# Two transformer blocks on one core: the plain sum of squares at the block boundary moved from VectorE to GpSimd

## The chip, the cores and the metric

The kernel runs on one core of one Trainium2 chip. The metric is the device time of one execution in microseconds, and the time of a kernel is the median of its runs. The trace comes from one further, profiled execution of the same program.

## The reference, cut to what matters

The program computes two blocks in a row on a sequence of 1024 tokens with 1024 features. The first ends with an MLP and a final norm; its output goes straight into the first norm and the input projection of the second:

```python
def first_block(x, ..., final_norm_g):
    ...
        x = x + jnp.square(jax.nn.relu(h2 @ w_up[l])) @ w_down[l]
    return rms_norm(x, final_norm_g)

def second_block(x, norm1_g, w_in, b_in, ...):
    ...
        h = _rmsnorm(x, norm1_g[l])
        z = h @ w_in[l] + b_in[l]
        q, k, v, c_a, c_b, g_a, g_b = jnp.split(z, splits, axis=-1)
        ...
```

Two norms thus stand one behind the other. With r1 the inverse root of the mean of x², the first gives y = x · r1 · final_norm_g, and the second needs the mean of y², which is r1² times the mean of x² · final_norm_g². Each token needs two sums over the features: one of the plain squares x², and one of the squares weighted by final_norm_g².

## The kernel before

**Layout.** Activations are kept with features on the 128 partitions and tokens along the free axis: `x_t` is eight slices (`KT` = 8) of 128 features by 1024 tokens. A weight tile is 128 output features of a matrix. All products are float32 split in two parts (`hi` and `lo`, three matmuls for each pair), so one weight tile against one activation slice is 3 x 2 matmuls of 128x512, and a whole tile is 48. `product(n, slot, first_bank, ...)` on TensorE is one such tile; it waits until GpSimd has split tile `n` (`weight_split`) and ends by raising `tile_done`.

**Weights.** SyncE loads tile `n` into `w_raw` slot n mod 2. GpSimd's `split` makes `w_hi` with a cast (line 975) and `w_lo` with a subtraction (line 983), and waits beforehand for `tile_done` at n - 1, since the tile two back must have left the slot. `weight_stream` writes out the order of all tiles for both of them: a part of it is a list of tiles written out, then a hardware loop (`Fori`), then another list. Tiles `T_CB` to `T_CB + 3` (`CT` = 4) are the first of the second block; before, they are a hardware loop of two rounds with two tiles each.

**Squares at the boundary.** ScalarE squares the eight slices of `x_t` in the order `BLOCK_ORDER`: square 0 goes straight into `sq_sum`, squares 1 to 4 into `sq`, 5 to 7 into `sq_rest`; each raises `sq_ready`. VectorE then adds in this order, 15 instructions of 128x1024:

- `sum_gained(0, 0)`: `sq_sum_gain` = square 0 times its weight (line 3055). It must read `sq_sum` before that is overwritten.
- `sum_plain(e, ...)` for e = 1 to 7: `sq_sum` += square e (line 3049).
- `sum_gained(e, ...)` for e = 1 to 7: `sq_sum_gain` += square e times its weight (line 3058).

Each raises `sq_summed`, and each waits for the one before it, since the sum is in place.

**TensorE at the boundary.** `sum_features` multiplies a sum by a matrix of ones, two float32 matmuls of 128x512 (line 1140), which adds over the partitions. The order is written by hand:

```python
            product(T_CB + 1, 1, 2, h_hi, h_lo, range(KT // 2))
            sum_features(sq_sum, SUMS_MIX2 + KT, 4)
            product(T_CB + 1, 1, 2, h_hi, h_lo, range(KT // 2, KT))
            sum_features(sq_sum_gain, SUMS_MIX2 + 2 * KT - 1, 6)

            pe.wait_ge(mean_log, 3)
            product(T_CB + 2, 0, 4, h_hi, h_lo)
            pe.wait_ge(block_mean, 1)
            product(T_CB + 3, 1, 6, h_hi, h_lo)
```

The plain sum goes to banks 4 and 5, where ScalarE takes its logarithm (line 2231, `mean_log`), from which it makes the inverse roots; the weighted sum goes to banks 6 and 7, and VectorE multiplies it in at line 3076 (`block_mean`). Engines run their own instructions in program order, so a wait of TensorE holds everything behind it.

Of the kernel before, what the change touches and what calls it, by code (L numbers as in the profile page):

```python
# [26 lines left out]
ACT = mybir.ActivationFunctionType  # L27
# [162 lines left out]
SUMS_MIX1 = 0  # L190
SUMS_MLP = SUMS_MIX1 + 2 * (KT - 1)
SUMS_MIX2 = SUMS_MLP + KT - 1
SUMS_FFN = SUMS_MIX2 + 2 * KT - 1
SUMS_OUT = SUMS_FFN + KT - 1


# [13 lines left out]
def two_blocks(nc, dram, out):  # L210
    ctx = ExitStack()
    with ctx:
# [253 lines left out]
        def by_group(tile):  # L466
# [160 lines left out]
         product_added, product_taken) = (q_gate, f_ready, kd_start, g_gate, qd_start, v_ready, kd_turned, kd_tok_ready,  # L627
                                          update_done, o_done, o_sq)
        group_joined = [o_mean, o_inv]
        factors_loaded, direct_loaded, rest_loaded, sums_loaded = (x_loaded[j:j + 2] for j in range(0, KT, 2))  # L630

        block = ctx.enter_context(nc.Block())
# [41 lines left out]
        def weight_stream(eng, step, step_pair, mlp_down, begun=0):  # L674

            parts = [
                ((pool_tiles + head_tiles(0))[begun:], HEADS - 1, lambda i: head_tiles(i + 1), []),  # L680
                ([columns(dram["w_out"], d * P) for d in ORDER], 0, None, []),
                (mlp, mlp_up),
                (mlp_down,),
                ([], CT // 2, lambda i: [columns(w_in2, CB2 + i * 2 * P + j * P) for j in range(2)], []),
                (pair_tiles(0)[0:2], PAIRS - 1, lambda p: pair_tiles(p)[2:4] + pair_tiles(p + 1)[0:2],
                 pair_tiles(PAIRS - 1)[2:4] + gate_tiles(0)),
                ([], KT - 1, lambda i: gate_tiles(i + 1), []),
                ([], KT // 2, lambda i: [branches(i * 2 * P + j * P) for j in range(2)], []),
                ([columns(dram["w_out_2"], d * P) for d in ORDER], 0, None, []),
                (ffn, ffn_up),  # L690
                (ffn_down(0), FFN_CHUNKS - 2, lambda i: ffn_down(i + 1), ffn_down(FFN_CHUNKS - 1)),
            ]
            n, skipped = begun, 0
            for part in parts:
                if len(part) == 1:
                    part[0]()
                    continue
                if len(part) == 2:

                    stage, tiles = part  # L700
                    assert (n, skipped) == (stage.tile, stage.skipped)
                    for q in range(2):
                        step_pair(stage, n, stage.pair + q, q, tiles(q))
                        n += 2
                    with eng.Fori(0, stage.pairs // 2 - 1) as i:
                        for s in range(2):
                            step_pair(stage, i * 4 + (n + 2 * s), i * 2 + (stage.pair + 2 + s), s, tiles(i * 2 + (2 + s)))
                    n += 2 * stage.pairs - 4
                    skipped += 16 * stage.pairs
                    continue  # L710
                ahead, count, body, behind = part
                for halves in ahead:
                    step(n, n % 2, halves, skipped)
                    n += 1
                if count:
                    size = len(body(0))
                    assert size % 2 == 0 and n % 2 == 0
                    with eng.Fori(0, count) as i:
                        for j, halves in enumerate(body(i)):
                            step(i * size + (n + j), j % 2, halves, skipped)  # L720
                    n += count * size
                for j, halves in enumerate(behind):
                    step(n, n % 2, halves, skipped)
                    n += 1
            assert n == T_END
# [28 lines left out]
        def join_corner(eng, g, j):  # L754

            rest, corner = down_sum(g, j, "t1"), output_at(g, j, "c22")
            if j == 0:
                eng.wait_ge(sums_loaded[g], 16 + 96)
            eng.tensor_tensor(rest, rest, corner, ALU.add).then_inc(group_joined[g], 1)
            eng.wait_ge(group_joined[g], HEADS + 12 + 2 * j + 1)  # L760
            eng.tensor_tensor(rest, rest, down_sum(g, j, "t3"), ALU.add).then_inc(group_joined[g], 1)

        def joined_before(j, name):

# [169 lines left out]
        def _(pool):  # L934
# [7 lines left out]
            def split(n, slot, _, skipped):  # L942

                pool.wait_ge(weight_loaded[slot], arrived(n, slot, skipped))
                hi, lo = w_hi[:, slot, :], w_lo[:, slot, :]
                if isinstance(n, int) and n == T_END - 1:

                    pool.wait_ge(tile_done, T_END - 4)
                    hi, lo = w_hi_last[:, :], w_lo_last[:, :]
                elif isinstance(n, int) and n == T_HEADS:  # L950

                    pool.wait_ge(x_turned, 2 * KT)
                    hi, lo = w_hi_first[:, :], w_lo_first[:, :]
                elif isinstance(n, int) and n == T_OUT1 + 1:

                    pool.wait_ge(tile_done, n - 1)
                    pool.wait_ge(level_moved, (HEADS - 1) * LEVELS + 3)
                elif isinstance(n, int) and n in (T_OUT1 + 2, T_OUT1 + 3):

                    pool.wait_ge(mix_split, KT - 1)  # L960
                    for read in ((k_ready, q_ready), (v_turned, sg_ready))[n - T_OUT1 - 2]:
                        pool.wait_ge(read, HEADS)
                    hi, lo = w_out_parts[n - T_OUT1 - 2]
                elif isinstance(n, int) and n == T_DOWN2:

                    pool.wait_ge(tile_done, n - 2)
                elif isinstance(n, int) and n == T_DOWN2 + 1:

                    pool.wait_ge(tile_done, T_DOWN2)
                elif not isinstance(n, int) or n >= 2:  # L970

                    pool.wait_ge(tile_done, n - 1)

                pool.sem_inc(wait_passed, 1)
                pool.tensor_copy(hi, w_raw[:, slot, :]).then_inc(weight_hi, 1)  # L975
                pool.wait_ge(weight_hi, n + 1)
                if isinstance(n, int) and n == T_POOL + 1:

                    pool.wait_ge(h_ready, H_MIX1 + KT)
                elif isinstance(n, int) and n == T_HEADS:  # L980

                    pool.wait_ge(sq_summed, SUMS_MIX1 + 3)
                pool.tensor_tensor(lo, w_raw[:, slot, :], hi.bitcast(F32), ALU.subtract).then_inc(weight_split, 1)  # L983

            def split_pair(stage, n, q, s, _):

# [111 lines left out]
        def _(pe):  # L1098
# [33 lines left out]
                                             start=(k == 0 and j == 0), stop=(k == 1 and j == 2))  # L1132
                    last.then_inc(down_done if g < 7 else tile_done, 1)

            def sum_features(src, summed, first_bank):


                pe.wait_ge(sq_summed, summed)
                for t in range(2):
                    last = pe.matmul(psum[:, first_bank + t, :], ones[:, :], src[:, t * HALF:(t + 1) * HALF],  # L1140
                                     start=True, stop=True)
# [416 lines left out]
                    order=BLOCK_ORDER)  # L1558
            pe.wait_ge(product_added, HEADS + product_read(at_last + 7)[1])
            product(T_CB + 1, 1, 2, h_hi, h_lo, range(KT // 2))  # L1560
            sum_features(sq_sum, SUMS_MIX2 + KT, 4)
            product(T_CB + 1, 1, 2, h_hi, h_lo, range(KT // 2, KT))
            sum_features(sq_sum_gain, SUMS_MIX2 + 2 * KT - 1, 6)

            pe.wait_ge(mean_log, 3)
            product(T_CB + 2, 0, 4, h_hi, h_lo)
# [226 lines left out]
        def _(act):  # L1793
# [421 lines left out]

            def block_square(e):

                dst = sq_sum[:, :] if e == 0 else sq[:, e % SQ_SLOTS, :] if e <= SQ_SLOTS else sq_rest[:, e - SQ_SLOTS - 1, :]
                act.activation(dst, x_t[:, BLOCK_ORDER[e], :], ACT.Square).then_inc(sq_ready, 1)

            act.wait_ge(product_added, HEADS + product_read(SEVENS + 7)[1])
            for e in range(4):
# [300 lines left out]
        def _(dve):  # L2523
# [515 lines left out]
            def block_lo(e):  # L3039
                lo_part(BLOCK_ORDER[e], gain_both[:, BLOCK_ORDER[e]:BLOCK_ORDER[e] + 1], H_MIX2, nth=e)  # L3040

            def block_squared(e):
                return sq[:, e % SQ_SLOTS, :] if e <= SQ_SLOTS else sq_rest[:, e - SQ_SLOTS - 1, :]

            def sum_plain(e, done):
                dve.wait_ge(sq_ready, 3 * KT + e + 1)

                dve.wait_ge(sq_summed, SUMS_MIX2 + done)
                dve.tensor_tensor(sq_sum[:, :], sq_sum[:, :], block_squared(e), ALU.add).then_inc(sq_summed, 1)  # L3049

            def sum_gained(e, done):
                dve.wait_ge(sq_ready, 3 * KT + e + 1)
                gain = gain_sq[:, BLOCK_ORDER[e]:BLOCK_ORDER[e] + 1]
                if e == 0:
                    dve.tensor_scalar(sq_sum_gain[:, :], sq_sum[:, :], gain, None, ALU.mult).then_inc(sq_summed, 1)
                else:
                    dve.wait_ge(sq_summed, SUMS_MIX2 + done)
                    dve.scalar_tensor_tensor(sq_sum_gain[:, :], block_squared(e), gain, sq_sum_gain[:, :],
                                             ALU.mult, ALU.add).then_inc(sq_summed, 1)

            for e, name in enumerate(OUTPUTS):
                add_output(1, 0, name)
# [2 lines left out]
                add_output(1, 1, name)  # L3065
            for e in range(4, KT):
                block_lo(e)
            sum_gained(0, 0)
            for e in range(1, KT):
                sum_plain(e, e)  # L3070
            for e in range(1, KT):
                sum_gained(e, e + KT - 1)

            dve.wait_ge(block_rinv1, 1)
            dve.wait_ge(norm_summed, 4)
# [423 lines left out]
```

## Time and profile before

| what | value |
|---|---|
| median of 3 runs | 2483.41 us (2482.99 to 2485.0) |
| profiled execution: its time | 2482.41 us |
| profiled execution: its span | 2480.4 us |
| TensorE busy | 2432.5 us, 98% |
| VectorE busy | 1814.0 us, 73% |
| GpSimd busy | 1258.9 us, 51% |
| ScalarE busy | 888.1 us, 36% |
| TensorE's share of the chain that ended last | 87% |
| VectorE's share of that chain | 7% |
| boundary of the blocks | about 1118 to 1185 us |

The span runs from the first to the last instruction in the trace; the time of the same execution is 2.0 us more, and the median of the other runs 1.0 us above that. Busy shares are means over stages that have different limits. The chain that ended last is followed back from the last instruction, at each step to what released it.

### The profile page before, as it was taken

The page shows a single profiled execution, that of the slowest core. Times are in us where ns is not written, and L with a number is a line of the kernel's source. Part 1 is how long each engine was busy: PE and PEld are TensorE (multiplying, and loading weights), DVE is VectorE, ACT ScalarE, POOL GpSimd, SP SyncE. Part 2 cuts the span into 40 slices and gives each one's busy share as a digit, 9 for nine tenths or more (in the row PEclk, how much of TensorE's full clock was granted, in tenths as well). Part 3 has the DMA queues.
Part 4 walks back from the last instruction along what each step waited for, and adds up shares of the span by engine and source line. Part 5 has one row for each costly group of instructions (what it writes and reads, how often), then busy time and mean ns, then how long its engine had stood idle before and what let it go on. Part 6 is the DMA issues. An engine that isn't in the chain of part 4 may idle for free.

```text
span 2480.4 us, 37674 instructions
## 1 busy us (share of the span) xinstructions
PE 2432.5 (98%) x13915; PEld 1995.8 (80%) x13915; DVE 1814.0 (73%) x1885; ACT 888.1 (36%) x1227; POOL 1258.9 (51%) x737
## 2 busy tenths in 40 slices
PE   8999999999999899998999999999999999999998
PEld 8788887878888688886777788888878888887887
DVE  6755556776566688888777888353889999987666
ACT  5333335353333543314233331311354545431003
POOL 2322222379886677763322223332389999962324
PEclk9999999999999999999999999999999999999999
DMA  6111112245544644422311111113312222243222
GB/s 223 37 41 34 34 34 96 101 150 169 180 166 183 232 157 140 152 94 79 101 41 40 40 30 48 51 43 136 111 60 93 76 84 90 80 158 113 93 85 93
DMA packets 237005, 245.98 MB, mean 99 GB/s; under 512 B 16720, under 2 KB 202747, under 8 KB 232059
## 3 DMA queue, kind: packets, MB, share of 16 engines
q1 hardware_dynamic: 204196, 154.90, 20.0%
q10 hardware_dynamic: 32726, 89.97, 9.6%
q8 instruction: 53, 0.87, 0.1%
q14 instruction: 30, 0.24, 0.0%
HBM read 179.82 MB, written 66.79 MB: 99 GB/s over the span
## 4 chain that ended last, share of the span: by engine, by line
PE 87%; DVE 7%; ACT 2%; DMA 1%; issue 1%; ACTq 0%; SPq 0%; DVEq 0%; POOL 0%; POOLq 0%
PE psum L1112 29%; PE psum L1402 26%; PE psum L1522 12%; PE psum L1131 8%; PE psum L1667 3%; PE psum L1151 2%; PE psum L1237 1%; PE psum L1176 1%; PE psum L1599 1%; DVE sq_sum L2828 1%; PE psum L1580 1%; PE psum L1778 1%; DVE sq_sum L3049 0%; DMA x_t<-x_spill 0%; PE psum L1297 0%
## 5 line engine op out<-in xcount | busy, mean ns | idle before, releaser
L975 POOL CAST w_hi<-w_raw 128x1024 fp32r<-128x1024 f32 x104 | 119.0, 1144 | 936.2 <-issue 439.2
L1112 PE MATMUL psum<-h_hi,w_hi 128*128 128x512 f32 x1040 | 333.3, 402 | 2.7 <-DVE x_t L2986 1.6
L1112 PE MATMUL psum<-h_lo,w_hi 128*128 128x512 f32 x1040 | 321.9, 391 | 0.0
L1112 PE MATMUL psum<-h_hi,w_lo 128*128 128x512 f32 x1040 | 320.8, 390 | 0.0
L983 POOL TENSOR_TENSOR w_lo<-w_raw,w_hi 128x1024 fp32r<-128x1024 f32 x104 | 267.3, 2570 | 11.5 <-DVE h_lo L2546 3.2
L1112 PEld LDWEIGHTS psum<-h_hi,w_lo 128*128 128x128 f32 x1040 | 195.5, 188 | 42.1
L1112 PEld LDWEIGHTS psum<-h_lo,w_hi 128*128 128x128 f32 x1040 | 195.5, 188 | 41.8
L1112 PEld LDWEIGHTS psum<-h_hi,w_hi 128*128 128x128 f32 x1040 | 189.6, 188 | 43.7 <-issue 6.7
L3112 DVE SCALAR_TENSOR_TENSOR conv_t<-u_t,cols,conv_t 128x1024 f32<-128x1024 f32 x120 | 179.6, 1496 | 2.4
L2864 DVE TENSOR_TENSOR x_t<-x_t,psum 128x512 f32<-128x512 f32 x160 | 109.0, 685 | 74.2 <-PE psum L1131 73.3
L1032 POOL TENSOR_TENSOR ffn_s_lo<-ffn_s_sum,ffn_s_hi 128x512 fp32r<-128x512 f32 x84 | 159.0, 1922 | 7.0 <-POOL ffn_s_sum L1018 3.8
L1131 PE MATMUL psum<-ffn_hi,w_hi 128*128 128x512 f32 x320 | 124.7, 390 | 3.0 <-DVE x_t L2864 3.0
L1131 PE MATMUL psum<-ffn_lo,w_hi 128*128 128x512 f32 x320 | 124.5, 389 | 0.0
L1131 PE MATMUL psum<-ffn_hi,w_lo 128*128 128x512 f32 x320 | 124.5, 389 | 0.0
L1032 POOL TENSOR_TENSOR mlp_s_lo<-mlp_s_sum,mlp_s_hi 128x512 fp32r<-128x512 f32 x60 | 95.5, 1622 | 11.6 <-ACT mlp_s_hi L2009 11.6
L1402 PE MATMUL psum<-ffn_t_hi,ffn_s_hi 128*128 128x512 f32 x252 | 98.0, 389 | 0.0
L1402 PE MATMUL psum<-ffn_t_lo,ffn_s_hi 128*128 128x512 f32 x252 | 98.0, 389 | 0.0
L1402 PE MATMUL psum<-ffn_t_hi,ffn_s_lo 128*128 128x512 f32 x252 | 98.0, 389 | 0.0
L1522 PE MATMUL psum<-down_part_hi,down_hi_odd 128*128 128x512 f32 x228 | 88.7, 389 | 0.0
L1522 PE MATMUL psum<-down_part_lo,down_hi_odd 128*128 128x512 f32 x228 | 88.7, 389 | 0.0
L1522 PE MATMUL psum<-down_part_hi,down_lo_odd 128*128 128x512 f32 x228 | 88.7, 389 | 0.0
L2979 DVE TENSOR_TENSOR down_x<-down_x,psum 128x512 f32<-128x512 f32 x90 | 60.7, 680 | 31.4 <-PE psum L1522 18.3
(531 smaller groups left out, 6378.7 us busy)
## 6 DMA issues: line engine op xcount, KB each, us to landing
w_raw<-in_w_in SPq DMA_DIRECT2D x124, 256.0 KB, 3.0
w_raw<-in_w_up SPq DMA_DIRECT2D x76, 256.0 KB, 3.6
act_parts<-mlp_a ACTq DMA_DIRECT2D x30, 512.0 KB, 4.0
act_parts<-act_mixed ACTq DMA_DIRECT2D x15, 1024.0 KB, 4.0
down_part_raw<-act_parts SPq DMA_DIRECT2D x15, 1024.0 KB, 5.1
down_part_raw<-act_parts SPq DMA_DIRECT2D x15, 768.0 KB, 5.2
ffn_raw<-in_w_up SPq DMA_DIRECT2D x44, 256.0 KB, 3.3
ffn_rows<-ffn_gate ACTq DMA_DIRECT2D x22, 512.0 KB, 2.6
```

The costliest lines, as they stand in the source:

```text
L975: pool.tensor_copy(hi, w_raw[:, slot, :]).then_inc(weight_hi, 1)
L983: pool.tensor_tensor(lo, w_raw[:, slot, :], hi.bitcast(F32), ALU.subtract).then_inc(weight_split, 1)
L1032: done = pool.tensor_tensor(lo[:, :], full[c], hi[:, :].bitcast(F32), ALU.subtract)
L1112: last = pe.matmul(psum[:, first_bank + t, :], w, a[:, k, t * HALF:(t + 1) * HALF], start=(k == order[0] and j == 0), stop=(k == order[-1] ...
L1131: last = pe.matmul(psum[:, 4 + g % 4, :], w, a[k][:, t * HALF:(t + 1) * HALF], start=(k == 0 and j == 0), stop=(k == 1 and j == 2))
L1151: last = pe.transpose(psum[:, dst_bank + c // 4, (c % 4) * P:(c % 4 + 1) * P], block_in, ident[:, :])
L1402: last = pe.matmul(psum[:, bank, :], w, a[:, :], start=start and kk == part[0] and j == 0, stop=stop and kk == part[-1] and j == 2, skip_g ...
L1522: done = pe.matmul(psum[:, bank, :], w, b, start=first and i == 0 and k == 0, stop=last and i == len(window) - 1 and k == 2)
L1667: last = pe.matmul(psum[:, bank + t, :], w, a[:, t * HALF:(t + 1) * HALF], start=(k == 0 and j == 0), stop=(k == 3 and j == 2))
L2864: dve.tensor_tensor(x_d, x_d, psum[:, 4 + g % 4, :], ALU.add).then_inc(down_added, 1)
L2979: dve.tensor_tensor(total, total, psum[:, down_bank(p), :], ALU.add).then_inc(product_added, 1)
L3112: dve.scalar_tensor_tensor(acc, u_t[:, c % 2, tap:tap + SEQ], w, acc, ALU.mult, ALU.add)\
```

## The change

Seven additions (the plain ones) leave VectorE and are made by GpSimd, in the function `sum_squares`, which stands in GpSimd's order between the split of tile `T_CB + 1` and that of tile `T_CB + 2`. So that the split of one tile can be told from the others there, the four tiles are written out and no longer looped. VectorE's weighted sums count on a semaphore of their own (`gain_summed`, which is `sg_ready` used again, and stood at `HEADS`); GpSimd starts behind the first of them.

```diff
-SUMS_FFN = SUMS_MIX2 + 2 * KT - 1
+SUMS_FFN = SUMS_MIX2 + KT - 1
...
+        gain_summed = sg_ready
...
-                ([], CT // 2, lambda i: [columns(w_in2, CB2 + i * 2 * P + j * P) for j in range(2)], []),
+                ([columns(w_in2, CB2 + d * P) for d in range(CT)], 0, None, []),
...
+        def block_squared(e):
+
+            return sq_sum[:, :] if e == 0 else sq[:, e % SQ_SLOTS, :] if e <= SQ_SLOTS else sq_rest[:, e - SQ_SLOTS - 1, :]
...
+                elif isinstance(n, int) and n == T_CB + 2:
+
+                    sum_squares()
+                    pool.wait_ge(tile_done, n - 1)
...
+            def sum_squares():
+
+                pool.wait_ge(gain_summed, HEADS + 1)
+                for e in range(1, KT):
+                    pool.wait_ge(sq_ready, 3 * KT + e + 1)
+                    if e >= 2:
+                        pool.wait_ge(sq_summed, SUMS_MIX2 + e - 1)
+                    pool.tensor_tensor(sq_sum[:, :], sq_sum[:, :], block_squared(e), ALU.add).then_inc(sq_summed, 1)
...
-            def sum_features(src, summed, first_bank):
+            def sum_features(src, summed, first_bank, by=sq_summed):
...
-                pe.wait_ge(sq_summed, summed)
+                pe.wait_ge(by, summed)
...
-            sum_features(sq_sum, SUMS_MIX2 + KT, 4)
+            sum_features(sq_sum, SUMS_MIX2 + KT - 1, 4)
             product(T_CB + 1, 1, 2, h_hi, h_lo, range(KT // 2, KT))
-            sum_features(sq_sum_gain, SUMS_MIX2 + 2 * KT - 1, 6)
+            sum_features(sq_sum_gain, HEADS + KT, 6, gain_summed)
...
-            def sum_plain(e, done):
-                dve.wait_ge(sq_ready, 3 * KT + e + 1)
-
-                dve.wait_ge(sq_summed, SUMS_MIX2 + done)
-                dve.tensor_tensor(sq_sum[:, :], sq_sum[:, :], block_squared(e), ALU.add).then_inc(sq_summed, 1)
...
-            def sum_gained(e, done):
+            def sum_gained(e):
                 dve.wait_ge(sq_ready, 3 * KT + e + 1)
                 gain = gain_sq[:, BLOCK_ORDER[e]:BLOCK_ORDER[e] + 1]
                 if e == 0:
-                    dve.tensor_scalar(sq_sum_gain[:, :], sq_sum[:, :], gain, None, ALU.mult).then_inc(sq_summed, 1)
+                    dve.tensor_scalar(sq_sum_gain[:, :], sq_sum[:, :], gain, None, ALU.mult).then_inc(gain_summed, 1)
                 else:
-                    dve.wait_ge(sq_summed, SUMS_MIX2 + done)
+                    dve.wait_ge(gain_summed, HEADS + e)
                     dve.scalar_tensor_tensor(sq_sum_gain[:, :], block_squared(e), gain, sq_sum_gain[:, :],
-                                             ALU.mult, ALU.add).then_inc(sq_summed, 1)
+                                             ALU.mult, ALU.add).then_inc(gain_summed, 1)
...
-            sum_gained(0, 0)
-            for e in range(1, KT):
-                sum_plain(e, e)
+            sum_gained(0)
             for e in range(1, KT):
-                sum_gained(e, e + KT - 1)
+                sum_gained(e)
```

GpSimd's instructions at the boundary, before. The loop runs twice, so it stands for tiles `T_CB` to `T_CB + 3`; the names in brackets are the semaphores that a row waits for:

```order
L718 UNCONDITIONAL_BRANCH
L718 ISA
L972 REGISTER_ALU [waits weight_loaded_0]
L975 CAST w_hi<-w_raw 128x1024 [waits tile_done]
L976 REGISTER_ALU
L983 TENSOR_TENSOR w_lo<-w_raw,w_hi 128x1024 [waits weight_hi]
L975 CAST w_hi<-w_raw 128x1024 [waits weight_loaded_1,tile_done]
L976 REGISTER_ALU
L983 TENSOR_TENSOR w_lo<-w_raw,w_hi 128x1024 [waits weight_hi]
L718 REGISTER_ALU
L718 COMPARE_AND_BRANCH
```

The same place now, with the four tiles written out:

```order
L984 CAST w_hi<-w_raw 128x1024 [waits weight_loaded_0,tile_done]
L992 TENSOR_TENSOR w_lo<-w_raw,w_hi 128x1024 [waits weight_hi]
L984 CAST w_hi<-w_raw 128x1024 [waits weight_loaded_1,tile_done]
L992 TENSOR_TENSOR w_lo<-w_raw,w_hi 128x1024 [waits weight_hi]
L1001 TENSOR_TENSOR sq_sum<-sq_sum,sq 128x1024 [waits sq_ready,sg_ready,weight_loaded_0]
L1001 TENSOR_TENSOR sq_sum<-sq_sum,sq 128x1024 [waits sq_summed,sq_ready] x3
L1001 TENSOR_TENSOR sq_sum<-sq_sum,sq_rest 128x1024 [waits sq_summed,sq_ready] x3
L984 CAST w_hi<-w_raw 128x1024 [waits tile_done]
L992 TENSOR_TENSOR w_lo<-w_raw,w_hi 128x1024 [waits weight_hi]
L984 CAST w_hi<-w_raw 128x1024 [waits weight_loaded_1,tile_done]
L992 TENSOR_TENSOR w_lo<-w_raw,w_hi 128x1024 [waits weight_hi]
```

Seven additions stand ahead of the split of tile `T_CB + 2`, and the register and branch instructions are gone.

VectorE's instructions at the boundary, before:

```order
L3055 TENSOR_SCALAR sq_sum_gain<-sq_sum,gain_sq 128x1024 [waits sq_ready]
L3049 TENSOR_TENSOR sq_sum<-sq_sum,sq 128x1024 [waits sq_summed,sq_ready] x4
L3049 TENSOR_TENSOR sq_sum<-sq_sum,sq_rest 128x1024 [waits sq_summed,sq_ready] x3
L3058 SCALAR_TENSOR_TENSOR sq_sum_gain<-sq,gain_sq,sq_sum_gain 128x1024 [waits sq_summed,sq_ready] x4
L3058 SCALAR_TENSOR_TENSOR sq_sum_gain<-sq_rest,gain_sq,sq_sum_gain 128x1024 [waits sq_summed,sq_ready] x3
```

And now:

```order
L3063 TENSOR_SCALAR sq_sum_gain<-sq_sum,gain_sq 128x1024 [waits sq_ready]
L3066 SCALAR_TENSOR_TENSOR sq_sum_gain<-sq,gain_sq,sq_sum_gain 128x1024 [waits sg_ready,sq_ready] x4
L3066 SCALAR_TENSOR_TENSOR sq_sum_gain<-sq_rest,gain_sq,sq_sum_gain 128x1024 [waits sg_ready,sq_ready] x3
```

The seven plain additions are gone from VectorE, and the weighted ones follow straight on the first. On TensorE no instruction moves; the weighted `sum_features` waits for the other semaphore.

## Rows read from the trace of the kernel before

**Rows 1.** The page: busy us of each engine, its share of the span, instructions.

```profile
PE 2432.5 (98%) x13915; PEld 1995.8 (80%) x13915; DVE 1814.0 (73%) x1885; ACT 888.1 (36%) x1227; POOL 1258.9 (51%) x737
```

**Rows 2.** Waits of TensorE: who waited for whom, total us, times, longest.

```profile
PE psum L1140 <- DVE sq_sum L3049: 2.9, 1, 2.9
PE psum L1140 <- DVE sq_sum_gain L3058: 2.9, 1, 2.9
```

**Rows 3.** Timeline of TensorE at the boundary: start, length, instruction, idle before it.

```profile
1145.98 0.61 PE L1112 MATMUL psum<-h_hi,w_lo 128*128 128x512 f32 x2
1149.50 1.98 PE L1140 MATMUL psum<-sq_sum,ones 128*128 128x512 f32 x4 [2.90 <-DVE sq_sum L3049]
1150.92 1.03 PE L1112 MATMUL psum<-h_hi,w_hi 128*128 128x512 f32 x2
...
1155.88 0.61 PE L1112 MATMUL psum<-h_lo,w_hi 128*128 128x512 f32 x2
1156.33 0.61 PE L1112 MATMUL psum<-h_hi,w_lo 128*128 128x512 f32 x2
1159.80 1.98 PE L1140 MATMUL psum<-sq_sum_gain,ones 128*128 128x512 f32 x4 [2.85 <-DVE sq_sum_gain L3058]
1161.22 1.02 PE L1112 MATMUL psum<-h_hi,w_hi 128*128 128x512 f32 x2
```

**Rows 4.** Timeline of VectorE at the boundary.

```profile
1136.68 0.74 DVE L3055 TENSOR_SCALAR sq_sum_gain<-sq_sum,gain_sq 128x1024 f32<-128x1024 f32 x1
...
1149.55 5.45 DVE L3058 SCALAR_TENSOR_TENSOR sq_sum_gain<-sq,gain_sq,sq_sum_gain 128x1024 f32<-128x1024 f32 x4
...
1161.89 1.22 DVE L3076 TENSOR_TENSOR rinv<-rinv,psum 128x1024 f32<-128x1024 f32 x1 [2.15 <-PE psum L1140]
```

**Rows 5.** The chain that ended last: single plain additions, then TensorE: start, length, what.

```profile
1138.86 1.24 DVE sq_sum L3049
...
1141.52 1.94 DVE sq_sum L3049
...
1143.55 3.25 DVE sq_sum L3049
...
1161.79 62.60 PE psum L1112 x276
```

**Rows 6.** Timeline of GpSimd at the boundary: splits of tiles T_CB + 1 and T_CB + 2.

```profile
1129.69 2.40 POOL L983 TENSOR_TENSOR w_lo<-w_raw,w_hi 128x1024 fp32r<-128x1024 f32 x1
1141.33 1.04 POOL L975 CAST w_hi<-w_raw 128x1024 fp32r<-128x1024 f32 x1 [9.24 <-PE psum L1112]
1142.45 3.25 POOL L983 TENSOR_TENSOR w_lo<-w_raw,w_hi 128x1024 fp32r<-128x1024 f32 x1
```

**Rows 7.** Timelines of GpSimd and VectorE, both adding 128x512 tiles at once.

```profile
1102.62 1.73 POOL L759 TENSOR_TENSOR down_sum_t<-down_sum_t,x_t 128x512 f32<-128x512 f32 x1
...
1101.43 1.78 DVE L746 TENSOR_TENSOR down_x<-down_sum_t,down_x 128x512 f32<-128x512 f32 x1
1103.13 1.77 DVE L748 TENSOR_TENSOR down_sum_t<-down_sum_t,down_sum_t 128x512 f32<-128x512 f32 x1
```

**Rows 8.** Line 983 over the whole span: shortest, median, longest in ns.

```profile
L983 POOL TENSOR_TENSOR w_lo<-w_raw,w_hi x104: 2352/2405/3497, 7.5 to 2429.3; 128x1024 fp32r<-128x1024 f32 x104
```

**Rows 9.** Timeline of ScalarE: the logarithm of the plain sum.

```profile
1151.52 1.12 ACT L2231 ACTIVATE rinv<-psum,eps 128x1024 f32<-128x1024 f32 x1 [14.14 <-PE psum L1140]
```

**Rows 10.** Stretches: length, PE, PEld, DVE, ACT, POOL busy (x instructions), granted clock, DMA, GB/s.

```profile
818.00:820.00 2.00, 0.00 (x0) 0.00 (x0) 0.00 (x0) 1.50 (x2) 1.27 (x2) 0.50 0.99 366
...
826.00:828.00 2.00, 2.00 (x8) 1.58 (x7) 2.00 (x3) 0.75 (x2) 0.00 (x0) 0.70 0.79 279
...
1146.60:1149.50 2.90, 0.00 (x1) 0.00 (x1) 2.63 (x3) 0.00 (x0) 0.00 (x0) 1.00 0.61 181
```

**Rows 11.** Timeline of TensorE behind its longest wait; seven matmuls start from 824.01 on.

```profile
824.01 0.80 PE L1522 MATMUL psum<-down_part_hi,down_hi_first 128*128 128x512 f32 x1 [8.32 <-DVE down_x L2979]
...
827.16 0.41 PE L1522 MATMUL psum<-down_part_lo,down_hi_first 128*128 128x512 f32 x1
```

More of the change, by code:

```diff
@@ L2216, in block_square @@
             def block_square(e):
-                dst = sq_sum[:, :] if e == 0 else sq[:, e % SQ_SLOTS, :] if e <= SQ_SLOTS else sq_rest[:, e - SQ_SLOTS - 1, :]
-                act.activation(dst, x_t[:, BLOCK_ORDER[e], :], ACT.Square).then_inc(sq_ready, 1)
+                act.activation(block_squared(e), x_t[:, BLOCK_ORDER[e], :], ACT.Square).then_inc(sq_ready, 1)
             act.wait_ge(product_added, HEADS + product_read(SEVENS + 7)[1])
@@ L3040, in block_lo @@
                 lo_part(BLOCK_ORDER[e], gain_both[:, BLOCK_ORDER[e]:BLOCK_ORDER[e] + 1], H_MIX2, nth=e)
-            def block_squared(e):
-                return sq[:, e % SQ_SLOTS, :] if e <= SQ_SLOTS else sq_rest[:, e - SQ_SLOTS - 1, :]
-            def sum_plain(e, done):
-                dve.wait_ge(sq_ready, 3 * KT + e + 1)
-                dve.wait_ge(sq_summed, SUMS_MIX2 + done)
-                dve.tensor_tensor(sq_sum[:, :], sq_sum[:, :], block_squared(e), ALU.add).then_inc(sq_summed, 1)
-            def sum_gained(e, done):
+            def sum_gained(e):
                 dve.wait_ge(sq_ready, 3 * KT + e + 1)
```

## The prediction

> **What bounds the kernel now.** I read the page first: TensorE is busy for 98% of the span [rows 1], so a saving counts only where TensorE waits, and anything that makes TensorE wait longer counts in full. The waits of TensorE say where the two sums of the boundary matter: it waits 2.9 us for the plain sum and 2.9 us for the weighted one [rows 2]. The timeline of TensorE gives the clock times [rows 3]. The last pair of matmuls ahead of the plain sum starts at 1145.98 and is over at about 1146.60; the ones-matmuls start at 1149.50; half a tile follows from 1150.92; its last pair starts at 1156.33, and the next instruction waits until 1159.80; tile `T_CB + 2` starts at 1161.22. That is the end on which my sum rests, since from there the chain that ended last runs on TensorE alone to 1161.79 + 62.60 = 1224.39 [rows 5].
>
> The reader should see that all there is to win at this place is the 2.90 and the 2.85 us, 5.75 together, or 0.23% of the time, and only if both sums come in time. The weighted sum is late because VectorE does 15 additions in a row. Take the seven plain ones from it and its wait goes. But the plain sum is wanted first, and that is the one that is given to GpSimd.
>
> **The change part by part.**
>
> *The start.* The first weighted operation on VectorE ends at 1136.68 + 0.74 = 1137.42 [rows 4], and nothing in front of it is moved. GpSimd must wait for it. It is free by then, since its split of tile `T_CB + 1` ends at 1129.69 + 2.40 = 1132.09 [rows 6].
>
> *One addition on GpSimd.* No addition of 128x1024 in plain float32 stands on GpSimd in this trace. The nearest row is the subtraction of line 983, of the same width with two inputs in SBUF: 2405 ns median, 2352 at the shortest [rows 8]. On VectorE one addition takes 1.24 us and starts 1.33 after the one before, since from 1138.86 to 1141.52 there are two steps [rows 5]. So GpSimd is slower by a factor of 1.8 even when undisturbed: seven take at least 7 x 2.40 + 7 x 0.08 between them = 17.4 us, against 7 x 1.33 = 9.3 before.
>
> *Both engines at once.* The seven weighted operations of VectorE now run beside them, and the trace shows what that does. At 1142.45 GpSimd's subtraction takes 3.25 us in place of 2.40, and the plain addition that VectorE starts at 1143.55 takes 3.25 in place of 1.24 [rows 5, 6]. The ends tell how: VectorE's earlier addition ends at 1141.52 + 1.94 = 1143.46, GpSimd's subtraction at 1145.70, which is 2.24 later, and VectorE's next at 1146.80, which is 1.10 later. They take turns, each blocked while the other runs. The 128x512 additions show the same for several turns in a row: VectorE's start 1.70 us apart, at 1.78 each, and end 0.55 behind one of GpSimd's [rows 7]. A turn of both at 128x1024 is thus 2.24 + 1.10 = 3.34 us.
>
> The Trainium skill says this too (SBUF — State Buffer, Who interferes with whom): a VectorE instruction with two SBUF inputs and a GpSimd instruction that reads SBUF exclude each other for the whole instruction. By that rule, the trace agrees, and it speaks against this change: splitting two additions over these two engines runs nothing in parallel. The rule alone would have the undisturbed lengths add to 2.40 + 1.24 = 3.64 a turn; the rows say 3.34, and I take the rows.
>
> *When the plain sum is done.* VectorE's second weighted operation starts at 1137.53, as its second operation did before, and I let it come first: 1.28 us, from 5.45 us for four [rows 4], to 1138.81. Then come seven turns of GpSimd and six of VectorE: 7 x 2.24 + 6 x 1.10 = 22.3 us, to 1161.1. If GpSimd wins the first turn it is 1137.6 + 2.40 + 6 x 3.34 = 1160.0. I take 1161.1, because VectorE's wait is for its own semaphore. The upper bound takes undisturbed lengths in full: 1138.81 + 7 x 2.40 + 6 x 1.28 = 1163.3.
>
> *TensorE.* Its wait at the plain sum starts at 1146.60 as now and lasts to 1161.1, 14.5 us in place of 2.90. Behind it: ones-matmuls 1.42 (1149.50 to 1150.92), half a tile 5.86 (1150.92 to 1156.33, plus 0.45 for the last pair), then the weighted sum, which VectorE has ready by about 1159, so nothing is waited, and another 1.42. Tile `T_CB + 2` starts at 1161.1 + 8.7 = 1169.8 in place of 1161.22: **+8.6 us**.
>
> *The clock.* In the 2.90 us wait the granted clock stays at 1.00, 2.4 GHz. In TensorE's longest wait of this trace, 8.32 us, it stands at 0.50, 1.2 GHz, and comes back only after the work has started again: 0.70 over 826 to 828 [rows 10]. From 824.01 to 827.16 seven matmuls start [rows 11], 0.45 us each, where at full clock a pair takes 0.45 (1155.88 to 1156.33 in [rows 3]); 3.15 - 7 x 0.225 = 1.6 us lost. A wait of 14.5 us is longer, so I expect the same fall and the same price: **+1.5 us**, between 0 (the clock holds) and 3 (twice the row).
>
> *What the wait passes on.* The split of tile `T_CB + 2` stands behind the additions on GpSimd, and the load of the tile after next behind that split. It takes 1.04 + 2.40 and a little, to about 1164.8, and TensorE wants it at 1169.8: hidden by 5 us; had it no cover it would cost 3.6. The logarithm starts 2.02 us after the ones-matmuls and ends 3.14 after them [rows 9], well within the 8.7. VectorE's multiplication at line 3076 comes 0.67 us behind the start of `T_CB + 2` [rows 4], and all that follows keeps its distance to it. The register and branch instructions that leave the loop are hidden under GpSimd's 9.24 us of idle time before its cast [rows 6]; I count them at nothing. The seven additions that leave VectorE also gain nothing beyond the 2.85, since VectorE waits there for TensorE anyway.
>
> *The sum.* 8.6 + 1.5 = +10.1 us. Against the profiled execution's own 2482.41 that is 2492.5; the median stands 1.0 us above that execution, so I forecast **2493.5 us**. A change of 0.2% is 5.0 us, and below it I call two times of this kernel equal; this is 0.41%.
>
> **The rivals.**
>
> *A. GpSimd and VectorE don't hinder each other here.* For it: VectorE's operation is another one than in the rows, with a scalar per partition, and GpSimd's is an addition. Against it: turns show in every pair above. Then the sum is ready at 1137.6 + 17.4 = 1155.0, `T_CB + 2` starts at 1163.7, +2.5, with the clock's 1.5 (the wait is 8.4, as long as the row's): +4.0, 2487.4. This is also what the Trainium skill gives by itself (GPSIMD Engine Reference, Engine selection), which has GpSimd about twice as slow on two inputs.
>
> *B. GpSimd keeps its turn.* If the next addition is issued before VectorE gets in, GpSimd is done at 1155.0 and VectorE makes its seven until 1155.0 + 7 x 1.38 = 1164.7 (5.45 for four and the gaps between them). TensorE then waits 8.4 us for the plain sum and again at the weighted one, and `T_CB + 2` starts at 1164.7 + 1.4 = 1166.1: +4.9 and 1.5, 2489.8. Against it, GpSimd has 0.08 us between dependent additions, and VectorE stands ready in them.
>
> *C. VectorE keeps its turn.* It is done at 1147.3 and GpSimd starts then: 1147.3 + 17.4 = 1164.7, +12.2 and 1.5, 2497.1. Against it is the same gap, on the other side.
>
> *D. It gets faster.* One mechanism only: GpSimd adds fast enough. `T_CB + 2` starts earlier than before only if the plain sum is ready by 1161.22 - 8.74 = 1152.5, so an addition and its gap must take under 14.9 / 7 = 2.1 us. The shortest row is 2352 ns [rows 8]. Even at VectorE's own 1.24 us and undisturbed, all that is won is 5.75, just at the bound of 0.2%.
>
> *E. The delay is taken up behind.* A later wait that doesn't hang on TensorE would absorb it. For it speaks little: from `T_CB + 2` to 1224.39 the chain is TensorE alone. It would give some 2485.
>
> **How the numbers follow.** My forecast gets 0.70, A 0.07, B 0.08, C 0.07, D 0.02, E 0.04, and 0.02 is for what I don't see. My own case spans 2491 (GpSimd first, the clock holding: 7.5 above) to 2497.2 (upper bound of the turns, 2.2 more, with some of the clock's). B and C add 2489.8 and 2497.1. From 2488.5 to 2498 I hold 0.70 + 0.08 + 0.07 = 0.85 of which a little is lost at the edges. Slower by over 0.2% are my case, B and C: 0.85; within 0.2% are A, E and half of the unseen: 0.12; faster is D and the rest: 0.03.
>
> **What the profile after would show.** On GpSimd, seven additions of 128x1024 from about 1137.6 with starts 3.3 us apart, ending at about 1161. On VectorE, seven weighted operations starting 3.3 apart, most of them 3.2 us long. TensorE's wait for the weighted sum gone, and one of about 14.5 us for the plain sum on GpSimd, with the granted clock at 0.50 in its second part and for about 3 us behind it. All later stages as long as before. Additions at 2.4 us would mean A or B, and which of them VectorE's lengths tell; a clock of 1.00 throughout takes away the 1.5. I would be wrong in sign only if the additions took less than 2.1 us.

## The result

The changed kernel takes 2491.89 us in the median of 6 runs (2490.51 to 2495.39), against 2483.2 us for 6 runs of the kernel before (2480.55 to 2485.0). The ratio is 1.0037, with a 95% interval of 1.0026 to 1.0048: slower by 8.7 us, where 10.1 were forecast. A second measurement, on another occasion, gave 2492.44 against 2484.21 us, a ratio of 1.0033 (1.0022 to 1.0043).

The page of the changed kernel answers to [rows 1]. TensorE's busy time is nearly the same (1.3 us more); VectorE has 7 instructions fewer and GpSimd 7 more:

```profile
span 2488.8 us, 37636 instructions
PE 2433.8 (98%) x13915; PEld 1996.5 (80%) x13915; DVE 1812.4 (73%) x1878; ACT 889.5 (36%) x1227; POOL 1279.8 (51%) x744
```

VectorE lost seven additions of 1.2 us and its busy time fell by 1.6 us only. That is the first sign that what remained there got longer. The waits of TensorE (who waited for whom, total us, times, longest) answer to [rows 2]:

```profile
PE psum L1158 <- POOL sq_sum L1001: 13.2, 1, 13.2
PE psum L1540 <- DVE down_x L2996: 8.3, 1, 8.3
```

The wait for the weighted sum is gone from the list. The wait for the plain one grew from 2.9 to 13.2 us and is now the longest of the program. Timeline of TensorE at the boundary (start, length, instruction, idle before it), to be read beside [rows 3]:

```profile
1147.31 0.61 PE L1130 MATMUL psum<-h_hi,w_lo 128*128 128x512 f32 x2
1161.16 3.78 PE L1158 MATMUL psum<-sq_sum,ones 128*128 128x512 f32 x4 [13.24 <-POOL sq_sum L1001]
1163.95 1.84 PE L1130 MATMUL psum<-h_hi,w_hi 128*128 128x512 f32 x2
...
1171.04 1.88 PE L1158 MATMUL psum<-sq_sum_gain,ones 128*128 128x512 f32 x4
1172.35 1.03 PE L1130 MATMUL psum<-h_hi,w_hi 128*128 128x512 f32 x2
```

Tile `T_CB + 2` starts at 1172.35, and the weighted ones-matmuls have no wait in front of them. But the plain ones-matmuls take 2.79 us to the next start, where they took 1.42, and the first pair behind them is 1.84 long in place of 1.03. The chain that ended last (start, length, what) gives GpSimd's single additions, here the first four of seven:

```profile
1138.93 2.40 POOL sq_sum L1001
...
1141.47 3.19 POOL sq_sum L1001
...
1144.79 3.20 POOL sq_sum L1001
...
1148.13 3.15 POOL sq_sum L1001
...
1172.91 62.61 PE psum L1130 x276
```

Timeline of VectorE beside them, to be read against [rows 4]:

```profile
1138.05 0.74 DVE L3063 TENSOR_SCALAR sq_sum_gain<-sq_sum,gain_sq 128x1024 f32<-128x1024 f32 x1
1138.89 13.46 DVE L3066 SCALAR_TENSOR_TENSOR sq_sum_gain<-sq,gain_sq,sq_sum_gain 128x1024 f32<-128x1024 f32 x4
1152.45 9.73 DVE L3066 SCALAR_TENSOR_TENSOR sq_sum_gain<-sq_rest,gain_sq,sq_sum_gain 128x1024 f32<-128x1024 f32 x3
```

Only the first addition on GpSimd has its undisturbed 2.40 us; the others start 3.3 us apart. Four weighted operations of VectorE take 13.46 us where four took 5.45 [rows 4]. Before, its last three were these:

```profile
1155.10 4.65 DVE L3058 SCALAR_TENSOR_TENSOR sq_sum_gain<-sq_rest,gain_sq,sq_sum_gain 128x1024 f32<-128x1024 f32 x3
```

So the move did not even relieve VectorE at this place. With 15 operations it was done 1159.75 - 1137.42 = 22.3 us behind the end of the first; with the eight that are left it is done 1162.18 - 1138.79 = 23.4 us behind it. TensorE no longer waits for the weighted sum only because it asks for it so much later.

Last, stretches of 2 us (length, busy by engine, then the granted clock as third number from the end):

```profile
1150.00:1152.00 2.00, 0.00 (x0) 0.00 (x0) 2.00 (x1) 0.00 (x0) 1.86 (x2) 1.00 0.00 0
1152.00:1154.00 2.00, 0.00 (x0) 0.00 (x0) 1.90 (x2) 0.00 (x0) 2.00 (x1) 0.72 0.00 0
1154.00:1156.00 2.00, 0.00 (x0) 0.00 (x0) 1.90 (x2) 0.00 (x0) 1.86 (x2) 0.50 0.00 0
...
1166.00:1168.00 2.00, 2.00 (x9) 1.64 (x8) 0.00 (x0) 1.97 (x3) 0.00 (x0) 0.87 0.59 166
```

The clock falls to 0.50 (1.2 GHz) between 1152 and 1154, in the wait, and is back at 1.00 (2.4 GHz) only between 1166 and 1168. A mean of 0.87 over those 2 us means about 0.5 us more at the low level, so it lasted to about 1166.5, 5.4 us behind the restart at 1161.16.

**A measure that the rest of the program doesn't blur.** Executions of one and the same kernel differ by several microseconds (26 runs of the kernel before: 2480.89 to 2488.99), and the ten profiled executions shown here end the first weighted operation anywhere from 1137.42 to 1141.20. So beside the medians I use a distance within one execution: from the end of the first weighted operation on VectorE to the first matmul of the attention scores, which closes TensorE's long run behind the boundary. Before it is 1224.39 - 1137.42 = 86.97 us [rows 4, 5]; in the changed kernel 1172.91 + 62.61 - 1138.79 = 96.73. The boundary itself thus costs +9.76. Each distance is from one execution. The two profiles of the changed kernel differ by 0.3 us, and those of two kernels with the same work here (before, and written out only) by 0.65, so smaller differences say nothing.

### The profile page after: what moved, and what is told of

It is laid out like the page before. It is cut to its first block, busy times and chain, and to the rows that moved or that the text cites. A ratio compares the mean times of both kernels' runs of the same rounds, so it can differ in the third digit from the quotient of the medians.

```text
span 2488.8 us, 37636 instructions
## 1 busy us (share of the span) xinstructions
PE 2433.8 (98%) x13915; PEld 1996.5 (80%) x13915; DVE 1812.4 (73%) x1878; ACT 889.5 (36%) x1227; POOL 1279.8 (51%) x744
## 4 chain that ended last, share of the span: by engine, by line
PE 86%; DVE 6%; ACT 2%; issue 1%; DMA 1%; POOL 1%; ACTq 1%; SPq 0%; DVEq 0%; POOLq 0%
PE psum L1130 29%; PE psum L1420 25%; PE psum L1540 12%; PE psum L1149 8%; PE psum L1685 3%; PE psum L1169 2%; PE psum L1255 1%; PE psum L1617 1%; POOL sq_sum L1001 1%; PE psum L1194 1%; DVE sq_sum L2845 1%; PE psum L1598 1%; ACTq L2086 1%; PE psum L1796 1%; DMA x_t<-x_spill 0%
```

## The experiments

| kernel | median, us | before beside it | ratio, 95% interval | distance, us |
|---|---|---|---|---|
| before | 2483.2 | | | 86.97 |
| changed | 2491.89 | 2483.2 | 1.0037, 1.0026 to 1.0048 | 96.73 |
| changed, again | 2492.44 | 2484.21 | 1.0033, 1.0022 to 1.0043 | 96.45 |
| written out only | 2482.87 | 2484.12 | 0.9998, 0.9989 to 1.0007 | 86.32 |
| one after the other | 2495.88 | 2484.12 | 1.0043, 1.0029 to 1.0056 | 99.91 |
| filler | 2491.38 | 2484.12 | 1.0031, 1.002 to 1.0043 | 94.34 |
| sums later | 2480.47 | 2484.12 | 0.9982, 0.9973 to 0.9991 | 82.11 |
| sums later, split late | 2478.68 | 2484.21 | 0.9974, 0.9963 to 0.9985 | 81.96 |
| split late | 2486.9 | 2484.21 | 1.0011, 1.0002 to 1.002 | 90.85 |
| changed, sums later | 2489.13 | 2484.21 | 1.0017, 1.0007 to 1.0026 | 91.78 |

The ratio is worked out from all runs of both kernels and is not exactly that of the two medians. The theory is that of the prediction: GpSimd and VectorE take turns, so the plain sum is late, TensorE waits for it, and its clock falls.

### Written out only

```diff
-                ([], CT // 2, lambda i: [columns(w_in2, CB2 + i * 2 * P + j * P) for j in range(2)], []),
+                ([columns(w_in2, CB2 + d * P) for d in range(CT)], 0, None, []),
```

> The kernel before with the four tiles T_CB to T_CB + 3 written out and no longer looped; all additions stay on VectorE. My theory: the loop costs nothing on the path, so the time is that of before, within 0.1%, and tile T_CB + 2 starts as far behind the end of the first weighted operation as before (1161.22 - 1137.42 = 23.8 us). Rival: the 1.3 us by which the changed kernel already comes late to the boundary, and more behind it, are the price of writing out: 1.3 us or more above before.

No difference that the interval would show, and the distance is 0.65 us shorter. So the loop is worth nothing here that could be measured. The first weighted operation ends at 1137.57, where it was 1137.42 before and 1138.79 in the changed kernel, so the later arrival of the changed kernel is not the doing of the loop either. The profile held a surprise. TensorE at the plain sum, and the stretch behind it:

```profile
1149.60 3.54 PE L1140 MATMUL psum<-sq_sum,ones 128*128 128x512 f32 x4 [2.89 <-DVE sq_sum L3049]
...
1150.00:1152.00 2.00, 2.00 (x3) 0.77 (x3) 1.90 (x2) 0.00 (x0) 0.00 (x0) 0.50 0.00 0
```

The same wait of 2.9 us, in which the clock held before [rows 10], is followed here by a granted clock of 0.50. It cost nothing. TensorE came some 1.5 us later to the weighted sum, but its wait there shrank by 2.1 (0.72 us in place of 2.85), since the weighted sum was ready 0.6 us sooner too: GpSimd's next split, which waits for TensorE, began later and stood beside less of it.

### One after the other

```diff
                 else:
+                    if e == 1:
+                        dve.wait_ge(sq_summed, SUMS_MIX2 + KT - 1)
                     dve.wait_ge(gain_summed, HEADS + e)
```

> The changed kernel, but VectorE waits with its second weighted operation until GpSimd's seven additions are done, so the two never run at once. If taking turns is what makes the additions long, each of GpSimd's takes 2.40 us again, the plain sum is ready 17.3 us behind the end of the first weighted operation (22.3 in the changed kernel), TensorE waits some 8 us for it and again 2 to 3 us for the weighted one, and T_CB + 2 starts at about +31 us behind that end in place of 33.6: in all about 2 to 3 us less than the changed kernel. Rival: an addition of this kind on GpSimd takes 3.1 us by itself. Then the plain sum is ready as late as before and the weighted one another 12 us later: some 4 us or more above the changed kernel.

Half right. The chain that ended last gives the same additions of GpSimd, now alone, and VectorE's behind them:

```profile
1142.00 2.40 POOL sq_sum L1001
...
1144.54 2.40 POOL sq_sum L1001
...
1154.55 2.34 POOL sq_sum L1001
...
1159.04 3.20 DVE sq_sum_gain L3068
...
1163.72 1.30 DVE sq_sum_gain L3068
...
1168.60 3.18 DVE sq_sum_gain L3068
```

The lengths decide for the theory: 2.34 to 2.40 us each when VectorE stands still, 3.14 to 3.20 beside it (all but the first), same operation, same tiles. The whole did not come out as I expected, though. Tile `T_CB + 2` starts 35.3 us behind the end of the first weighted operation, where I had 31, and the distance is 3.2 us longer than in the changed kernel, not shorter. That is near what the rival gave, but its reason, long additions of GpSimd by themselves, is excluded by the lengths. I had reckoned with one split of GpSimd beside the weighted operations; both splits, of `T_CB + 2` and of `T_CB + 3`, now lie there (the two operations of 3.2 us), so that the seven take 1171.78 - 1156.97 = 14.8 us, where they took 10.2 before. TensorE waits 5.61 us a second time, and its clock falls a second time:

```profile
1156.93 3.78 PE L1158 MATMUL psum<-sq_sum,ones 128*128 128x512 f32 x4 [8.45 <-POOL sq_sum L1001]
...
1171.82 3.78 PE L1158 MATMUL psum<-sq_sum_gain,ones 128*128 128x512 f32 x4 [5.61 <-DVE sq_sum_gain L3068]
```

### Filler

```diff
+            for i in range(48):
+                pe.matmul(psum[:, 4 + i % 2, :], w_hi[:, 1, 0:P], h_hi[:, 0, 0:HALF], start=True, stop=True)
             sum_features(sq_sum, SUMS_MIX2 + KT - 1, 4)
```

> The changed kernel with 48 matmuls of 128x512 more on TensorE ahead of the ones-matmuls of the plain sum, into the banks that these overwrite; nothing uses their result. They take 10.9 us of the 13.2 us wait. If the fallen clock costs 2.5 us there, as the profile of the changed kernel says, the granted clock stays at 1.00 through the boundary and the time is 2.5 us below the changed kernel. Rival: the fallen clock costs nothing that counts (the logarithm or another step ends as late anyway), and the time is that of the changed kernel.

At the boundary this came out as expected. TensorE:

```profile
1163.74 1.98 PE L1158 MATMUL psum<-sq_sum,ones 128*128 128x512 f32 x4 [2.47 <-POOL sq_sum L1001]
1165.16 1.03 PE L1130 MATMUL psum<-h_hi,w_hi 128*128 128x512 f32 x2
...
1171.06 1.88 PE L1158 MATMUL psum<-sq_sum_gain,ones 128*128 128x512 f32 x4
1172.37 1.03 PE L1130 MATMUL psum<-h_hi,w_hi 128*128 128x512 f32 x2
```

From the plain ones-matmuls to tile `T_CB + 2` it is 8.63 us, against 11.19 in the changed kernel: 2.56 us are the price of the fallen clock. The distance shrinks by 2.4. The medians of the two kernels are 2491.38 and 2491.89, from different occasions; between those a gain of 2.4 can be neither shown nor denied.

### Sums later, on VectorE

```diff
-            product(T_CB + 1, 1, 2, h_hi, h_lo, range(KT // 2))
+            product(T_CB + 1, 1, 2, h_hi, h_lo, range(6))
             sum_features(sq_sum, SUMS_MIX2 + KT, 4)
-            product(T_CB + 1, 1, 2, h_hi, h_lo, range(KT // 2, KT))
-            sum_features(sq_sum_gain, SUMS_MIX2 + 2 * KT - 1, 6)
+            product(T_CB + 1, 1, 2, h_hi, h_lo, range(6, KT))

             pe.wait_ge(mean_log, 3)
-            product(T_CB + 2, 0, 4, h_hi, h_lo)
+            product(T_CB + 2, 0, 4, h_hi, h_lo, range(5))
+            sum_features(sq_sum_gain, SUMS_MIX2 + 2 * KT - 1, 6)
+            product(T_CB + 2, 0, 4, h_hi, h_lo, range(5, KT))
```

> The kernel before with all additions on VectorE as they were; only TensorE's order is changed: six of eight slices of tile T_CB + 1 ahead of the plain sum in place of four, and five slices of tile T_CB + 2 ahead of the weighted one in place of none. If TensorE's two waits are all that is to win here, and all that follows has enough room, both nearly vanish: about 4.5 us less than before (2478.7). Rival: VectorE's chain behind the sums, and not TensorE, sets the end of the stage, so the waits reappear at the next tiles or in the pairs loop: same as before.

The distance is 4.9 us shorter than before and the time 0.18% less (0.09 to 0.27%), some 3.7 us in the medians, where about 4.5 were expected. The two waits of 2.90 and 2.85 us [rows 3] are 0.18 and 0.71 here, with VectorE's instructions as they were:

```profile
1152.83 1.98 PE L1140 MATMUL psum<-sq_sum,ones 128*128 128x512 f32 x4 [0.18 <-DVE sq_sum L3050]
...
1165.09 1.98 PE L1140 MATMUL psum<-sq_sum_gain,ones 128*128 128x512 f32 x4 [0.71 <-DVE sq_sum_gain L3059]
```

### Split late, with and without the later sums

Both have the four tiles written out and this edit in GpSimd's `split`; the first also has the weighted ones-matmuls behind five slices of `T_CB + 2`, as above:

```diff
+                elif isinstance(n, int) and n == T_CB + 2:
+
+                    pool.wait_ge(sq_summed, SUMS_MIX2 + KT)
+                    pool.wait_ge(tile_done, n - 1)
```

> The kernel before, additions all on VectorE, the four tiles written out, and two edits: GpSimd waits with the split of tile T_CB + 2 until the plain sum is ready, and the weighted ones-matmuls stand behind five of eight slices of tile T_CB + 2 (the plain ones stay behind four slices of T_CB + 1). If GpSimd's split is what made the plain sum 2.9 us late, the plain sum is ready in under 9.5 us behind the first weighted operation (12.0 before), TensorE's wait for it is under 0.5 us, and the whole is 4.5 to 5.5 us below before, a little under the kernel with later sums alone (2480.5, 3.6 below before). Rival: VectorE's work is what it is, the split's price is paid in the weighted sum, and nothing is won over later sums alone.

> The kernel before with the four tiles written out and the split of tile T_CB + 2 behind the plain sum; TensorE's order as before. By the turns, the split takes from VectorE the same 2.7 us wherever it stands beside it: the plain sum comes 2.7 us sooner (wait under 0.5 in place of 2.9), the weighted one as late as before, tile T_CB + 2 starts 23 to 24 us behind the end of the first weighted operation as before (23.8), and the time is that of before within 0.1%. Rival: the two additions were slow for another reason, and the plain sum stays 12 us long.

Without the later sums, TensorE, VectorE, and GpSimd's two subtractions, of the splits of `T_CB + 2` and `T_CB + 3`:

```profile
1149.19 1.98 PE L1144 MATMUL psum<-sq_sum,ones 128*128 128x512 f32 x4 [0.20 <-DVE sq_sum L3053]
...
1163.94 3.78 PE L1144 MATMUL psum<-sq_sum_gain,ones 128*128 128x512 f32 x4 [7.29 <-DVE sq_sum_gain L3062]
...
1139.94 5.21 DVE L3053 TENSOR_TENSOR sq_sum<-sq_sum,sq 128x1024 f32<-128x1024 f32 x4
1145.25 3.89 DVE L3053 TENSOR_TENSOR sq_sum<-sq_sum,sq_rest 128x1024 f32<-128x1024 f32 x3
1149.24 8.00 DVE L3062 SCALAR_TENSOR_TENSOR sq_sum_gain<-sq,gain_sq,sq_sum_gain 128x1024 f32<-128x1024 f32 x4
...
1151.51 3.26 POOL L987 TENSOR_TENSOR w_lo<-w_raw,w_hi 128x1024 fp32r<-128x1024 f32 x1
...
1158.22 3.20 POOL L987 TENSOR_TENSOR w_lo<-w_raw,w_hi 128x1024 fp32r<-128x1024 f32 x1
```

The plain sum is ready 9.3 us behind the first weighted operation (1145.25 + 3.89 - 1139.83) in place of 12.0, so the split of GpSimd was what held it. But I had expected the time of before, and the kernel is slower by 0.11%, its distance 3.9 us longer. The split's price was moved into the weighted sum, as expected; what I missed is that TensorE, being sooner, frees the slot sooner, so that the split of `T_CB + 3` too falls beside the weighted operations, and that a wait of 7.29 us lets the clock fall.

With the later sums, that room is there. The plain sum is ready 9.3 us behind the first weighted operation again, and TensorE waits 0.21 us for it. But the distance is 81.96, against 82.11 for later sums alone: by this measure the rival is right, and the late split wins nothing by itself. The median of 2478.68 us, 0.26% under before (0.15 to 0.37%), is the lowest of all kernels here, but its interval overlaps that of later sums alone, so no preference between the two is shown.

### Changed, with the sums later

```diff
-            product(T_CB + 1, 1, 2, h_hi, h_lo, range(KT // 2))
+            product(T_CB + 1, 1, 2, h_hi, h_lo)
             sum_features(sq_sum, SUMS_MIX2 + KT - 1, 4)
-            product(T_CB + 1, 1, 2, h_hi, h_lo, range(KT // 2, KT))
-            sum_features(sq_sum_gain, HEADS + KT, 6, gain_summed)
...
-            product(T_CB + 2, 0, 4, h_hi, h_lo)
+            product(T_CB + 2, 0, 4, h_hi, h_lo, range(5))
+            sum_features(sq_sum_gain, HEADS + KT, 6, gain_summed)
+            product(T_CB + 2, 0, 4, h_hi, h_lo, range(5, KT))
```

> The changed kernel (GpSimd adds the plain squares) with TensorE's order changed: all of tile T_CB + 1 ahead of the plain sum, and five slices of tile T_CB + 2 ahead of the weighted one. TensorE then waits some 8 to 9 us for the plain sum in place of 13.2, and some 2 to 3 for the logarithm. If the additions on GpSimd are the cause of the loss, this stays above before by 4 to 6 us even with the order that suits it, and is 4 to 5 us below the changed kernel. Rival: the loss is only the place at which TensorE asks for the sum, and in this order the kernel is no slower than before.

```profile
1163.54 3.50 PE L1158 MATMUL psum<-sq_sum,ones 128*128 128x512 f32 x4 [7.84 <-POOL sq_sum L1001]
1168.23 0.73 PE L1130 MATMUL psum<-h_hi,w_hi 128*128 128x512 f32 x2 [1.21 <-ACT rinv L2248]
```

TensorE still waits 7.84 us and then 1.21 for the logarithm, both a little less than expected. The distance is 4.8 us above before and the time 0.17% (0.07 to 0.26%). This order halves the loss and no more; the same kind of order with all additions on VectorE is 9.7 us shorter in the distance (82.11 against 91.78).

### Changed, again

> The changed kernel as it is, beside the others of this call: about 2492, 8 to 9 us above before; tile T_CB + 2 starts 33.6 us behind the end of the first weighted operation, as in its first profile, give or take 1 us for which engine takes the first turn and for the clock.

2492.44 us, 8.2 above before, and tile `T_CB + 2` starts 1172.87 - 1139.59 = 33.28 us behind the end of the first weighted operation (33.56 in the first profile). GpSimd took the first turn here too.

## Why the prediction was right, point by point

- **The start and the first turn.** The first weighted operation ends at 1138.79 and GpSimd starts 0.14 us behind it. I let VectorE have the first turn, because it waits for its own semaphore, and this failed: in all four profiles in which both run at once GpSimd had it, at 2.40 to 2.41 us. It is the case for which I gave 1160.0 in place of 1161.1. The reason held as far as it went, since VectorE's operation is recorded as starting 0.04 us ahead of GpSimd's, in all four; yet it is the one that takes 3.51 us in place of 1.28:

```profile
1138.89 3.51 DVE L3066 SCALAR_TENSOR_TENSOR sq_sum_gain<-sq,gain_sq,sq_sum_gain 128x1024 f32<-128x1024 f32 x1
```

  Why a recorded start 0.04 us sooner does not win the turn, no run here shows.
- **One addition on GpSimd.** Taken as 2.40 us from a subtraction; measured alone as 2.34 to 2.40.
- **The turn.** Taken as 3.34 us; measured as 3.28 to 3.34 from start to start. The plain sum is ready 1161.11 - 1138.79 = 22.3 us behind the first weighted operation, where I had 1161.1 - 1137.42 = 23.7. The 1.4 are the first turn (1.1) and the slightly shorter others. The weighted sum, which I had ready 2 us ahead of the plain one, is ready 1.1 us behind it, again by the first turn. It cost nothing, since half a tile of TensorE stands between the two.
- **TensorE's wait.** 13.24 us, forecast 14.5: the same 1.3. The 2.85 us of the weighted sum were saved, as forecast.
- **The clock.** This is the term that was mis-sized. It fell and came back as forecast, but cost 2.5 us and not 1.5 (11.19 for what takes 8.70 at full clock; 2.56 by the filler). The row from which I priced it had the low clock for 3.15 us behind the restart, and here it lasted 5.4. So one row was too little to price it by: the second profile of the changed kernel has 1172.87 - 1161.94 = 10.93, a cost of 2.3. My upper bound of 3 held both.
- **What the wait passes on.** The split of `T_CB + 2` is over at 1163.16 + 2.35 = 1165.5, 6.8 us before TensorE wants it; the logarithm ended well before too. TensorE's run from there to the scores is unchanged: 62.61 us, against 62.60.
- **The sum.** +9.76 us at the boundary, forecast +10.1: 1.3 too much for the wait and 1.0 too little for the clock nearly cancel. That the total came so close is luck: each of the two terms is off by 1 us or more, and their sum by 0.3. The medians say +8.7; with an interval of 6.5 to 11.9 they agree with +9.76.
- **The rivals.** A (no hindrance) is excluded by the lengths beside VectorE and without it. B and C (one engine keeps its turn) are excluded by the even steps of 3.3 us. D needed additions under 2.1 us; none was. E (taken up behind) is excluded as far as the scores, where the 9.76 us are still whole, and the medians at the end leave room for about 1 us of it. The two profiled spans differ by 8.4 only: the changed kernel came to the boundary 1.4 us later, and won 2.2 us far behind it in a place that has nothing to do with the change (below). The remaining 0.5 us are not traced.

## What to carry to other kernels

When VectorE is late with a sum, moving two-input additions to GpSimd does not run them beside VectorE's own two-input operations: each put VectorE's operation back by about 1.9 us (from one start to the next 3.3 in place of 1.39), where VectorE itself needs 1.33 to do the addition. Look first whether the waiting engine can ask for the result later: here a few lines of TensorE's order won 3.7 us in the medians, and the move lost 8 to 9. And price a long wait of TensorE with what the clock loses behind it, 2.3 to 2.6 us here for one of 13.

## What the runs showed of the hardware

- **The clock after a short wait.** Behind waits of the same length, 2.90 us in the kernel before and 2.89 in the one written out, the granted clock was 1.00 throughout in one and 0.50 in the other. All waits of 5.6 us and more at the boundary were followed by 0.50. What decides in the short case stays open.
- **How long the low clock stays.** By the stretches of 2 us, it lasted from 3.1 us behind the restart (changed, sums later; wait of 7.84 us) to 5.9 (one after the other; second wait, 5.61 us). The longer time does not go with the longer wait. Those two stretches, in this order:

```profile
1166.00:1168.00 2.00, 1.03 (x2) 0.00 (x0) 0.00 (x0) 0.93 (x1) 2.00 (x2) 0.85 0.00 0
...
1176.00:1178.00 2.00, 2.00 (x7) 1.57 (x6) 0.94 (x1) 1.03 (x1) 0.00 (x0) 0.57 0.00 0
```

  The clock is low for 0.6 us of the first, to 1166.6 with the restart at 1163.54, and for 1.7 us of the second, to 1177.7 with the restart at 1171.82.
- **A race for the turn makes executions of one kernel differ.** In the second block's MLP, VectorE's subtraction for the down projection starts at nearly the same moment as GpSimd's split of a weight tile. VectorE's and GpSimd's rows before, then in the changed kernel:

```profile
2230.56 3.42 DVE L3325 TENSOR_TENSOR ffn_lo<-ffn_in,ffn_hi 128x1024 fp32r<-128x1024 f32 x1 [2.97 <-ACT ffn_hi L2419]
...
2230.52 2.37 POOL L983 TENSOR_TENSOR w_lo<-w_raw,w_hi 128x1024 fp32r<-128x1024 f32 x1
...
2241.13 1.23 DVE L3331 TENSOR_TENSOR ffn_lo<-ffn_in,ffn_hi 128x1024 fp32r<-128x1024 f32 x1 [2.79 <-ACT ffn_hi L2436]
...
2241.21 3.40 POOL L992 TENSOR_TENSOR w_lo<-w_raw,w_hi 128x1024 fp32r<-128x1024 f32 x1
```

  Before, GpSimd starts 0.04 us sooner and VectorE needs 3.42 us; in the changed kernel VectorE starts 0.08 us sooner, needs 1.23, and GpSimd needs 3.40. VectorE's operation stands on the chain that ended last, and TensorE waits 2.68 us behind it before and 0.37 in the changed kernel, so some 2.2 us of the time hang on who goes first. In ten profiles the operation took 3.2 to 3.4 us five times, each time with GpSimd recorded as starting sooner, and 1.2 to 1.7 five times, with VectorE sooner. Both happened with the change and without it, and in two executions of the changed kernel itself (1.23 and 3.30 us). The recorded start is no rule by itself, though: at the boundary the engine that started 0.04 us sooner had to wait. This is part of the scatter of the runs; that it is the largest part was not shown.
